# Group norm of a state-space scan: four squared tiles added on GpSimd before TensorE's row sum

## The chip, the cores and the metric

The kernel runs on one core of a Trainium2 chip. The metric is the device time of one execution in microseconds (us). The engines carry the names of the profile: PE is TensorE (matmuls, with weight loads as PEld), DVE is VectorE, ACT is ScalarE, POOL is GpSimd, SP is SyncE. Semaphores are the only thing that orders work on different engines.

## The reference, cut to what matters

The program is two transformer-like blocks on a sequence of 512 tokens of width 1024. The change sits in the second block, in the two-way state-space scan and the gated norm that follows it:

```python
v = (y * jax.nn.silu(z)).astype(jnp.float32).reshape(bsz, s, SSD_GROUPS, d // SSD_GROUPS)
v = v * lax.rsqrt(jnp.mean(v * v, axis=-1, keepdims=True) + EPS)
return (v.reshape(bsz, s, d) * g.astype(jnp.float32)).astype(y.dtype)
```

Here `y` is the scan's output (2048 channels), `SSD_GROUPS` is 4, and so each mean is over the 512 channels of one group. In the kernel channels lie on partitions and tokens along the free axis: a group is four tiles of 128 channels x 512 tokens, and the mean over channels is a sum over four tiles and over the 128 partitions of each.

## The kernel before

All matrix products go through one stream of weight units (128 x 1024). Each unit is split into a high and a low part, by ACT (`split_hi`, L342) and by DVE (`split_lo`, L348), and PE multiplies them in 48 matmuls of 256 columns (`product_tile`, L376).

The scan (`ssd_pe`, `ssd_act`, `ssd_dve`, `ssd_rows_dma`) makes 16 steps, f = 4 g + j, four groups g of four steps j, written out by hand on every engine. In a step PE computes the tiles x and z of step f (96 matmuls of L376), at j = 0 the four matmuls of `c_times_b` (L2376), at j = 1 of groups 1 to 3 `square_sum(g - 1)` (L2364), then `heads(f - 1)` (L2353, L2356), and transposes (L2391). `heads` multiplies with decay matrices in four chunks c, and waits for each.

The decay matrices of a step are made thus: POOL starts eight row copies from DRAM (L2315, four chunks, two heads each), DVE caps them (`cap`, L2492, one instruction per chunk), ACT takes exponentials (L2468, four activations per chunk), and DVE multiplies with a table (`times_cb`, L2498, two instructions per chunk). DVE also does the convolution (L2199), the output `v` (`out`, L2505 and L2508) and the group norm's scaling (L2514). Its order in step f is: convolution, `times_cb(f-1, 3)`, `cap(f, 0)`, `cap(f, 1)`, `split_lo`, `times_cb(f, 0)`, `out(f-1)`, `times_cb(f, 1)`, `cap(f, 2)`, `cap(f, 3)`, `split_lo`, at j = 2 the scaling, `times_cb(f, 2)`. ACT's `exponentials(f, 2)` wait for `cap(f, 2)`.

POOL's order in step f is: the copies of chunks 0 and 1, those of chunks 2 and 3 (each waits for PE to be done with the buffer, L2356), then for f = 1 to 12 the square of tile f - 1 (L2318, which waits for `v` from L2508), then for f = 8 to 15 the low part of the normed tile f - 8 (L2323). The squares of the last group are made on ACT (L2407).

`square_sum(g)` multiplies each squared tile with a matrix of ones and accumulates in one PSUM bank; ACT takes the inverse root there (L2411, L2413).

Of the kernel before, what the change touches and what calls it, by code (L numbers as in the profile page):

```python
# [20 lines left out]
ALU = mybir.AluOpType  # L21
# [176 lines left out]
def build(nc, dram, out):  # L198
    ctx = ExitStack()
    with ctx:  # L200
# [4 lines left out]
        def place(name, first, n, dtype):  # L205
            return first, n, nc.alloc_sbuf_tensor_at(name, [P, n, S], dtype, offset=base + first * S * 4)
        A = Slots(place("big", BIG, RES - BIG, F32), place("res_tmp", RES, N_SLOTS - RES, F32))
# [10 lines left out]
        ps = ctx.enter_context(nc.psum_tensor("ps", [P, 6, S], F32))  # L218
        ident = const[:, CONST["ident"]:CONST["ident"] + P]
        ones = const[:, CONST["ones"]:CONST["ones"] + P]  # L220
# [10 lines left out]
        def sem(name):  # L231
            return ctx.enter_context(nc.semaphore(name))
# [69 lines left out]
        def ev(name):  # L302
            name = SHARED.get(name, (name, 0))[0]
            if name not in s:
                s[name] = sem(name)
            return s[name]

        def nth(name, n):

            return n + SHARED[name][1]  # L310
# [47 lines left out]
        def product_tile(pe, u, t, hi, lo, blocks=(8,), n=S, ready=None, spare=None):  # L358


            pe.wait_ge(acc_free[t.bank], t.in_bank + 1)
            a, k, total = acc[t.bank], 0, sum(blocks)
            parts = [slice(at, at + HALF) for at in range(0, n, HALF)]
            for m in blocks:
                pe.wait_ge(lo_done, u.count + 1)
                for b in range(m):
                    if ready is not None:
                        pe.wait_ge(ev(ready[0]), ready[1] + k + 1)
                    wh = w_hi[:, u.slot, b * P:(b + 1) * P]
                    wl = w_lo[:, u.slot, b * P:(b + 1) * P]  # L370
                    for term, (w, x) in enumerate(((wh, hi), (wh, lo), (wl, hi))):
                        if spare is not None and (k, term) in SETTLE:
                            settle(pe, spare)
                        for h in parts:

                            mm = pe.matmul(a[:, h], w, AR[:, x + k, h], start=(k == 0 and w is wh and x == hi and h.start == 0),  # L376
                                           stop=(k == total - 1 and w is wl), skip_group_check=True)
                    k += 1
                mm.then_inc(units_used, 1)
                u = u + 1  # L380
# [1755 lines left out]
        XT, XTOK, VH, VL = 56, 58, 16, 32  # L2136
# [13 lines left out]
        def rows_buf(b):  # L2150
            return A[:, ROWS + 5 * b:ROWS + 5 * b + 5].rearrange("p b n -> p (b n)")
# [8 lines left out]
        def part(f, b, c):  # L2160
            rows, at = both(f, c)
            return rows[:, b, at:at + S + P]

        def back(f, b, c):
            return part(f, b, c)[:, 0:LENB[c]]

        def fore(f, b, c):
            return part(f, b, c)[:, LENB[c]:S + P]
# [129 lines left out]
        def ssd_rows_dma(pool):  # L2298
            rows = rows_buf(0)
            pool.wait_ge(ev("s_rows"), 8)  # L2300
            for c in range(CH):
                for r, at, n in ((slice(0, 32), FORE[c], LEN[c]), (slice(32, 64), BACK[c], LENB[c])):
                    pool.dma_start(SCR_ROWS[:, at:at + n], rows[r, at:at + n]).then_inc(ev("s_rows_out"), 16)
            pool.wait_ge(ev("s_rows_out"), 2 * CH * 16)
            pool.wait_ge(ev("s_rdiag"), nth("s_rdiag", 1))

            for f in range(SSD_TILES):
                for c in range(CH):

                    before = f - 1 if c < 2 else f  # L2310
                    for b in range(2):
                        if before >= 0:
                            pool.wait_ge(ev("s_pv"), 8 * before + 2 * c + b + 1)
                        src = SCR_ROWS[2 * f + b:2 * f + b + 1, BACK[c]:BACK[c] + S + P].to_broadcast([P, S + P])
                        pool.dma_start(part(f, b, c), src).then_inc(ev(row_in(f, c)), 16)  # L2315
                if 1 <= f <= POOL_SQ:
                    pool.wait_ge(ev("s_v"), f)
                    pool.tensor_tensor(A[:, VH + f - 1], A[:, VL + f - 1], A[:, VL + f - 1],  # L2318
                                       ALU.mult).then_inc(ev("s_vsq"), 1)
                if 8 <= f < 8 + POOL_LO:  # L2320
                    k = f - 8
                    pool.wait_ge(ev("s_vhi"), k + 1)
                    pool.tensor_tensor(AR[:, VL + k], A[:, VL + k], AR[:, VH + k].bitcast(F32),  # L2323
                                       ALU.subtract).then_inc(ev("s_vlo"), 1)


        POOL_SQ, POOL_LO = 12, 8

        def row_in(f, c):
            return f"s_row_in{f % 2}{c}" if c < 2 else f"s_row_in{c}"  # L2330

        def cb_bank(g, c):

            return (3, 4, 5, 0 if g else 1)[c]
# [3 lines left out]
        def ssd_pe(pe):  # L2338
            def heads(f, j, first=False):

                pe.wait_ge(ev("s_xtok"), f + 1)
                if not first or j >= 2:
                    pe.wait_ge(ev("s_v0"), f - 1)

                def x(b, c):
                    return A[:, XTOK + j % 2, c * P + 64 * b:c * P + 64 * b + 64]

                def o(b, lo, hi):
                    return ps[64 * b:64 * b + 64, j % 2, lo:hi]
                for c in range(CH):  # L2350
                    pe.wait_ge(ev("s_w"), 8 * f + (2 * c + 3))
                    for b in range(2):
                        pe.matmul(o(b, c * P, S), x(b, c), fore(f, b, c), start=(c == 0), stop=False,  # L2353
                                  skip_group_check=True)
                    for b in range(2):
                        pe.matmul(o(b, 0, LENB[c]), x(b, c), back(f, b, c),  # L2356
                                  start=False, stop=(c == 3), skip_group_check=True).then_inc(ev("s_pv"), 1)

            def square_sum(g):
                if g < GROUPS - 1:  # L2360
                    pe.wait_ge(ev("s_cb_rest"), 4 * g + 8)
                for k in range(4):
                    pe.wait_ge(ev("s_vsq"), 4 * g + (k + 1))
                    mm = pe.matmul(ps[:, 5], ones, A.at(VH, 4 * g + k), start=(k == 0), stop=(k == 3))  # L2364
                mm.then_inc(ev("s_vsum"), 1)

            def c_times_b(g, first):

                pe.wait_ge(ev("s_bg"), g + 1)
                if first:  # L2370
                    pe.wait_ge(ev("s_bc"), 2 * CH)
                    pe.wait_ge(ev("s_tab"), nth("s_tab", 2))
                for c in range(CH):
                    if c == 3 and not first:
                        pe.wait_ge(ev("s_v0"), 4 * g - 1)
                    pe.matmul(ps[:, cb_bank(g, c)], A[:, BG, c * P:(c + 1) * P], A.at(CT, g), start=True,  # L2376
                              stop=True).then_inc(ev("s_cbt"), 1)

            def group(g, first=False):
                for j in range(4):  # L2380
                    for m in range(2):
                        product_tile(pe, Units(UB["ssd"] + 2 * j + m, g, 8), Tiles(TB["ssd"] + 2 * j + m, g, 8), XH, XL)
                    if j == 0:
                        c_times_b(g, first)
                    if j == 1 and not first:
                        square_sum(g + (-1))
                    if j or not first:
                        heads(4 * g + (j - 1), (j - 1) % 4, first)
                    pe.wait_ge(ev("s_xt"), 4 * g + j + 1)
                    for c in range(CH):  # L2390
                        mm = pe.transpose(ps[:, 2, c * P:(c + 1) * P], A[:, XT + j % 2, c * P:(c + 1) * P], ident)  # L2391
                    mm.then_inc(ev("s_xtt"), 1)
            for g in range(GROUPS):
                group(g, g == 0)

            product_tile(pe, Units(UB["br_ssd"]), Tiles(TB["br_ssd"]), XH, XL)
            heads(SSD_TILES - 1, 3)
            square_sum(GROUPS - 1)

        def ssd_act(act):  # L2400
# [1070 lines left out]
```

## Time and profile before

| | |
|---|---|
| median of 3 runs | 2652.12 us (2649.25 to 2654.46) |
| profiled execution | 2653.07 us, its span 2650.9 us |
| busy, share of the span | PE 97%, DVE 61%, ACT 49%, POOL 4% |
| granted TensorE clock, mean | 0.989 |
| L2364 (square sum) | 32 matmul records of 592 ns |
| L2318 (squares on POOL) | 12 of 1549 ns |
| L2323 (low parts on POOL) | 8, median 1858 ns |

A matmul of 512 columns in this kernel's float32 leaves two records, so L2364's 32 records are 16 matmuls. Records overlap, as matmuls are pipelined: the time of a matmul is read from the start of one to the start of the next. The same holds for DVE, where an instruction starts a little before the one before it has ended. The scan lies between about 1440 and 1751 us of the span.

### The profile page before, as it was taken

What the parts mean: (1) busy time and instruction counts of PE and PEld (TensorE: products, weight loads), DVE (VectorE), ACT (ScalarE), POOL (GpSimd) and SP (SyncE); (2) the same over time, 40 slices, a digit from 0 to 9 for tenths busy, and PEclk for the clock granted to TensorE, in tenths of its full rate; (3) what the DMA queues carried; (4) which work ended last, traced back from release to release, by engine and by line L of the source; (5) the groups of instructions that cost most, each with busy time, mean ns of one, the idle gap of its engine ahead of it and who ended that gap; (6) DMA issues with size and microseconds to landing.
All of it is one profiled execution on the core that took longest, in us unless ns stands there. A gap on an engine that the chain in (4) does not pass through costs nothing.

```text
span 2650.9 us, 51120 instructions
## 1 busy us (share of the span) xinstructions
PE 2566.6 (97%) x20718; PEld 2368.5 (89%) x20718; DVE 1611.5 (61%) x2730; ACT 1295.4 (49%) x2175; POOL 115.2 (4%) x178
## 2 busy tenths in 40 slices
PE   8999999999998999999999998989999999999998
PEld 7976999999995799999989777779966998999998
DVE  6864666643688676664467998952475444544433
ACT  4556344432457554442365888742475333444422
POOL 0000000000000000000001333300000000000000
PEclk9999999999999999999999999999999999999999
DMA  4341233233231123333354666633211331333232
GB/s 166 109 105 19 64 106 102 96 104 104 96 112 49 33 82 101 98 96 120 98 197 136 203 195 193 196 97 100 91 48 62 99 119 54 94 100 95 95 104 72
DMA packets 76187, 279.04 MB, mean 105 GB/s; under 512 B 9802, under 2 KB 12010, under 8 KB 75488
## 3 DMA queue, kind: packets, MB, share of 16 engines
q1 hardware_dynamic: 62112, 217.42, 25.1%
q0 software_dynamic: 13888, 58.88, 7.7%
q8 instruction: 146, 2.39, 0.4%
q14 instruction: 41, 0.34, 0.0%
HBM read 267.03 MB, written 9.24 MB: 104 GB/s over the span
## 4 chain that ended last, share of the span: by engine, by line
PE 80%; DVE 12%; ACT 4%; issue 3%; DMA 1%; POOL 0%; DVEq 0%; SPq 0%; ACTq 0%
PE acc L376 59%; PE acc L565 4%; PE acc L407 3%; PE ps L565 3%; DVE big L2199 2%; DVE res_tmp L2498 1%; PE ps L407 1%; PE acc L2047 1%; DVE big L2829 1%; DVE w_lo L348 1%; DVE big L1851 1%; PE acc L1699 1%; PE ps L753 1%; DMA res_tmp<-scratch_rows 1%; PE ps L1080 1%
## 5 line engine op out<-in xcount | busy, mean ns | idle before, releaser
L376 PE MATMUL acc<-x_split,w_hi 128*128 128x256 f32 x6784 | 1054.6, 278 | 5.4 <-DVE big L2199 3.3
L376 PEld LDWEIGHTS acc<-x_split,w_hi 128*128 128x128 f32 x6784 | 900.8, 189 | 8.0 <-issue 7.4
L342 ACT ACTIVATE w_hi<-w_raw 128x1024 fp32r<-128x1024 f32 x369 | 389.1, 1056 | 562.0 <-PE acc L376 518.9
L376 PE MATMUL acc<-x_split,w_lo 128*128 128x256 f32 x3392 | 662.2, 277 | 0.0
L348 DVE TENSOR_TENSOR w_lo<-w_raw,w_hi 128x1024 fp32r<-128x1024 f32 x369 | 449.9, 1221 | 300.2 <-ACT w_hi L342 300.1
L376 PE MATMUL acc<-big_r,w_hi 128*128 128x256 f32 x3376 | 522.3, 277 | 0.8 <-DVE big_r L2882 0.8
L376 PEld LDWEIGHTS acc<-x_split,w_lo 128*128 128x128 f32 x3392 | 512.4, 188 | 0.0
L376 PEld LDWEIGHTS acc<-big_r,w_hi 128*128 128x128 f32 x3376 | 446.8, 188 | 1.7 <-DVE big_r L2882 0.9
L376 PE MATMUL acc<-big_r,w_lo 128*128 128x256 f32 x1688 | 329.2, 276 | 0.0
L376 PEld LDWEIGHTS acc<-big_r,w_lo 128*128 128x128 f32 x1688 | 254.4, 188 | 0.0
L1378 ACT ACTIVATE res_tmp<-acc,par 128x512 f32<-128x512 f32 x84 | 65.1, 774 | 135.1 <-PE acc L376 130.7
L1403 DVE SCALAR_TENSOR_TENSOR res_tmp<-acc,par,res_tmp 128x511 f32<-128x511 f32 x84 | 62.8, 748 | 87.4 <-ACT res_tmp L1378 87.2
L2468 ACT ACTIVATE res_tmp<-res_tmp 128x256 f32<-128x256 f32 (+3 forms) x192 | 91.1, 551 | 36.4 <-DVE res_tmp L2492 36.3
L2498 DVE TENSOR_TENSOR res_tmp<-res_tmp 128x640 f32<-128x640 f32 x96 | 81.7, 888 | 13.8 <-ACT res_tmp L2468 13.5
L565 PE MATMUL acc<-big_r,w_hi 128*128 128x256 f32 x432 | 78.0, 280 | 8.4 <-issue 8.3
L2199 DVE SCALAR_TENSOR_TENSOR big<-acc,par,big 128x510 f32<-128x510 f32 (+1 forms) x96 | 71.8, 748 | 12.8 <-ACT big L2189 10.1
L407 PE MATMUL acc<-big_r,w_hi 128*128 128x256 f32 x432 | 76.2, 281 | 0.7 <-DVE res_tmp L833 0.7
L565 PEld LDWEIGHTS acc<-big_r,w_hi 128*128 128x128 f32 x432 | 66.0, 190 | 9.4 <-issue 9.4
L1383 ACT ACTIVATE res_tmp<-res_tmp 128x512 f32<-128x512 f32 x44 | 27.9, 633 | 89.6 <-DVE small L1411 89.6
L581 ACT ACTIVATE w_hi<-w_sum 128x512 fp32r<-128x512 f32 x72 | 45.6, 633 | 52.2 <-DVE w_sum L602 52.2
L1406 DVE SCALAR_TENSOR_TENSOR res_tmp<-acc,par,res_tmp 128x510 f32<-128x510 f32 x84 | 62.9, 749 | 11.7 <-DVE res_tmp L1403 0.3
L407 PEld LDWEIGHTS acc<-big_r,w_hi 128*128 128x128 f32 x432 | 65.9, 188 | 1.5 <-DVE res_tmp L833 1.1
(403 smaller groups left out, 3558.5 us busy)
## 6 DMA issues: line engine op xcount, KB each, us to landing
w_raw<-in_stream SPq DMA_DIRECT2D x405, 512.0 KB, 3.5
res_tmp<-scratch_rows POOLq DMA_DIRECT2D x96, 320.0 KB, 5.1
big<-scratch_rows POOLq DMA_DIRECT2D x32, 320.0 KB, 5.7
scratch_bias<-res_tmp POOLq DMA_DIRECT2D x1, 2560.0 KB, 54.5
res_tmp<-in_x SPq DMA_DIRECT2D x2, 1024.0 KB, 6.7
res_tmp<-scratch_bias POOLq DMA_DIRECT2D x8, 256.0 KB, 4.1
scratch_x<-res_tmp POOLq DMA_DIRECT2D x1, 2048.0 KB, 8.0
scratch_kv<-big POOLq DMA_DIRECT2D x1, 2048.0 KB, 7.9
```

The source lines that it names most:

```text
L342: act.activation(w_hi[:, u.slot], w_raw[:, u.slot], ACT.Copy).then_inc(hi_done, 1)
L348: dve.tensor_tensor(w_lo[:, u.slot], w_raw[:, u.slot], w_hi[:, u.slot].bitcast(F32), ALU.subtract).then_inc(lo_done, 1)
L376: mm = pe.matmul(a[:, h], w, AR[:, x + k, h], start=(k == 0 and w is wh and x == hi and h.start == 0), stop=(k == total - 1 and w is wl), ...
L407: mm = pe.matmul(a[:, cols], w, AR[:, x + k, cols], start=(start and k == 0 and w is wh and x == hi), stop=(k == total - 1 and w is wl), s ...
L565: mm = pe.matmul(to, w[:, cols], st_x(stage, f, lo, k), start=(f in (0, 1, 5) and k == n == 0), stop=(k == 3 and n == 2 and f in (3, 5, 6) ...
L581: ins = act.activation(st_form(w_hi, n), x, ACT.Copy)
L1378: act.activation(x, acc[t.bank][:], ACT.Identity, bias=col(f"cb{f}", tile), scale=col(f"cw{f}", tile + 88)).then_inc(ev("conv_now"), 1)
L1403: dve.scalar_tensor_tensor(x[:, 1:S], a[:, 0:S - 1], col(f"cw{f}", tile + 44), x[:, 1:S], ALU.mult, ALU.add).then_inc(ev("conv_tap1"), 1)
L1406: dve.scalar_tensor_tensor(x[:, 2:S], a[:, 0:S - 2], col(f"cw{f}", tile), x[:, 2:S], ALU.mult, ALU.add).then_inc(acc_free[t.bank], 1)
L2199: ins = dve.scalar_tensor_tensor(o, i, col("cw2", m + 24 * j), o, ALU.mult, ALU.add)
L2468: ins = act.activation(w, w, ACT.Exp, bias=tab[:, 0, c, head:head + 1])
L2498: dve.tensor_tensor(w, w, cb, ALU.mult).then_inc(ev("s_w"), 1)
```

## The change

For groups 0 to 2, POOL, after it has squared tile f - 1, adds it to the group's first squared tile (in place), once for the second, third and fourth tile of each group. That is nine more instructions on POOL, each with a wait for POOL's own square. PE's `square_sum` of these groups then is one matmul where it was four. The semaphore `s_vsq` now counts seven steps for such a group (four squares, three sums), and the waits' values follow. The last group stays as it was.

```diff
                 if 1 <= f <= POOL_SQ:
                     pool.wait_ge(ev("s_v"), f)
+                    g, k = divmod(f - 1, 4)
                     pool.tensor_tensor(A[:, VH + f - 1], A[:, VL + f - 1], A[:, VL + f - 1],
                                        ALU.mult).then_inc(ev("s_vsq"), 1)
+                    if k:
+                        pool.wait_ge(ev("s_vsq"), 7 * g + 2 * k)
+                        pool.tensor_tensor(A[:, VH + 4 * g], A[:, VH + 4 * g], A[:, VH + f - 1],
+                                           ALU.add).then_inc(ev("s_vsq"), 1)
...
             def square_sum(g):
                 if g < GROUPS - 1:
                     pe.wait_ge(ev("s_cb_rest"), 4 * g + 8)
+                if g < POOL_SQ // 4:
+                    pe.wait_ge(ev("s_vsq"), 7 * g + 7)
+                    pe.matmul(ps[:, 5], ones, A.at(VH, 4 * g), start=True, stop=True).then_inc(ev("s_vsum"), 1)
+                    return
                 for k in range(4):
-                    pe.wait_ge(ev("s_vsq"), 4 * g + (k + 1))
+                    pe.wait_ge(ev("s_vsq"), 7 * g + (k + 1))
                     mm = pe.matmul(ps[:, 5], ones, A.at(VH, 4 * g + k), start=(k == 0), stop=(k == 3))
                 mm.then_inc(ev("s_vsum"), 1)
```

`POOL_SQ` is 12 and `POOL_LO` is 8. The steps f with an added sum are 2, 3, 4, 6, 7, 8, 10, 11 and 12.

## Rows read from the trace of the kernel before

**Rows 1.** Busy time of each engine (with instruction counts) over the scan.

```profile
1440.00:1751.00 311.00, 290.38 (x2153) 227.06 (x2152) 276.90 (x372) 248.28 (x435) 97.54 (x144) 0.97 0.59 186
```

**Rows 2.** Chain that ended last, within the scan: start us, us, what.

```profile
1529.32 3.43 PE ps L2364 x8
...
1652.69 12.09 PE acc L376 x96
...
1673.26 10.89 PE acc L376 x96
1684.15 3.43 PE ps L2364 x8
...
1693.08 7.10 DMA res_tmp<-scratch_rows
```

**Rows 3.** Waits in the scan: who waited for whom, us in total, times, longest.

```profile
PE ps L2353 <- DVE res_tmp L2498: 20.6, 11, 4.6
...
ACT res_tmp L2468 <- DVE res_tmp L2492: 36.3, 15, 3.0
```

**Rows 4.** Timeline of PE at square_sum(0): start, us, engine line op, form, count.

```profile
1529.16 3.59 PE L2364 MATMUL ps<-big,const 128*128 128x512 f32 x8
```

**Rows 5.** Timeline of PE at chunk 3 of heads(4), heads(8) and heads(12).

```profile
1535.96 0.39 PE L2353 MATMUL ps<-res_tmp,big 128*64 128x128 f32 x4
...
1610.32 0.44 PE L2353 MATMUL ps<-res_tmp,big 128*64 128x128 f32 x4 [0.61 <-DVE res_tmp L2498]
...
1690.80 0.39 PE L2353 MATMUL ps<-res_tmp,big 128*64 128x128 f32 x4
```

**Rows 6.** Timeline of DVE: pairs of times_cb and of cap, without and with POOL beside them.

```profile
1532.13 1.55 DVE L2498 TENSOR_TENSOR res_tmp<-res_tmp 128x640 f32<-128x640 f32 x2
...
1577.85 2.40 DVE L2498 TENSOR_TENSOR big<-big,res_tmp 128x640 f32<-128x640 f32 x2
...
1580.17 1.28 DVE L2492 TENSOR_TENSOR res_tmp<-res_tmp 128x512 f32<-128x512 f32 x2
...
1600.81 2.37 DVE L2492 TENSOR_TENSOR res_tmp<-res_tmp 128x512 f32<-128x512 f32 x2
```

**Rows 7.** Timeline of DVE: times_cb of chunk 3 of step 12.

```profile
1688.31 1.55 DVE L2498 TENSOR_TENSOR res_tmp<-res_tmp 128x640 f32<-128x640 f32 x2
```

**Rows 8.** Timeline of DVE: cap of chunks 2 and 3 in steps 2, 5 and 13.

```profile
1487.95 0.69 DVE L2492 TENSOR_TENSOR res_tmp<-res_tmp 128x512 f32<-128x512 f32 x1 [0.21 <-DMA res_tmp<-scratch_rows]
1489.33 0.69 DVE L2492 TENSOR_TENSOR res_tmp<-res_tmp 128x512 f32<-128x512 f32 x1 [0.69 <-DMA res_tmp<-scratch_rows]
...
1542.94 0.69 DVE L2492 TENSOR_TENSOR res_tmp<-res_tmp 128x512 f32<-128x512 f32 x1 [0.17 <-DMA res_tmp<-scratch_rows]
1544.47 0.69 DVE L2492 TENSOR_TENSOR res_tmp<-res_tmp 128x512 f32<-128x512 f32 x1 [0.85 <-DMA res_tmp<-scratch_rows]
...
1699.14 0.69 DVE L2492 TENSOR_TENSOR res_tmp<-res_tmp 128x512 f32<-128x512 f32 x1
1700.20 0.69 DVE L2492 TENSOR_TENSOR res_tmp<-res_tmp 128x512 f32<-128x512 f32 x1 [0.38 <-DMA res_tmp<-scratch_rows]
```

**Rows 9.** Timeline of POOL: a square, a low part behind a square, a low part alone.

```profile
1578.02 1.55 POOL L2318 TENSOR_TENSOR big<-big 128x512 f32<-128x512 f32 x1 [4.61 <-DVE big L2508]
...
1600.17 1.86 POOL L2323 TENSOR_TENSOR big_r<-big,big_r 128x512 fp32r<-128x512 f32 x1
...
1693.63 1.30 POOL L2323 TENSOR_TENSOR big_r<-big,big_r 128x512 fp32r<-128x512 f32 x1
```

**Rows 10.** Timeline of DVE: out(6), out(7), then out(10), out(11), their first instructions.

```profile
1576.46 0.74 DVE L2505 SCALAR_TENSOR_TENSOR big<-big,par,ps 128x512 f32<-128x512 f32 x1
...
1597.10 0.74 DVE L2505 SCALAR_TENSOR_TENSOR big<-big,par,ps 128x512 f32<-128x512 f32 x1
...
1654.95 0.74 DVE L2505 SCALAR_TENSOR_TENSOR big<-big,par,ps 128x512 f32<-128x512 f32 x1
...
1676.69 0.74 DVE L2505 SCALAR_TENSOR_TENSOR big<-big,par,ps 128x512 f32<-128x512 f32 x1
```

## The prediction

> **What bounds the kernel now.** I read the page first: PE is busy for 97% of the span, so taking matmuls away looks like time won. Then I read the scan alone. There PE is busy for 290.38 of 311 us and DVE for 276.90 [rows 1]: two engines close to full, and the question is which of them ends each step. The chain that ended last goes through both. It holds `square_sum(0)` at 1529.32 and `square_sum(2)` at 1684.15, with 3.43 us each, but nothing of `square_sum(1)` [rows 2]. The list of waits says why: PE waits in `heads` for DVE's `times_cb`, 11 times and 20.6 us in total [rows 3]. In a step that ends in such a wait PE's own speed is worth nothing, DVE's is worth all of it. ACT waits 15 times for DVE's `cap` (36.3 us) [rows 3]; so a delay of `cap(f, 2)` goes on to ACT and comes back in the next exponentials.
>
> **What is removed.** `square_sum` takes 3.43 us for four matmuls, less than the 3.59 us of its row, as the last record's end overlaps the next work [rows 2, 4]. One matmul is 3.43 / 4 = 0.86 us, three are 2.57 us, and three groups 7.7 us. That is the most the change can give. What of it reaches the end is read from chunk 3 of `heads` a few us later, in the same step, where PE meets DVE [rows 5]:
> - heads(4): PE comes at 1535.96 and doesn't wait. DVE was done at 1532.13 + 1.55 = 1533.68 [rows 6]. Cover: 2.28 us.
> - heads(8): PE already waits 0.61 us. Gain: none.
> - heads(12): PE comes at 1690.80, DVE was done at 1688.31 + 1.55 = 1689.86 [rows 7]. Cover: 0.94 us.
>
> What follows on the chain is a row copy that PE's progress releases, and DVE's `cap` behind it: in step 5 DVE waits 0.17 + 0.85 us for copies, in step 13 it waits 0.38 us [rows 8]. An earlier PE can't give back more than these two waits, 1.4 us in all, since DVE is next.
>
> **What is added.** Nine sums on POOL, each right behind a square. POOL itself has time: it waited 4.61 us for the tile before one square [rows 9]. The price is paid on DVE, which is seen in two rows. A pair of `times_cb` takes 1.55 us alone and 2.40 us with a square beside it: 0.85 us lost. A pair of `cap` takes 1.28 us alone and 2.37 us with a low part (L2323) beside it, which comes directly behind a square as the sum will: 1.09 us lost [rows 6]. These rows are also in steps that DVE ends, so I can see that the loss stays: from out(6) to out(7) there are 1597.10 - 1576.46 = 20.64 us with one POOL instruction in the step, and from out(10) to out(11), the same place one group later but with two, 1676.69 - 1654.95 = 21.74 us [rows 10]. The difference is 1.10 us.
>
> The sum has two different inputs and one output of 128 x 512, as the low part has, so I take 1.09 us for it. The bounds: 0.85 us from below (the square, which reads one tile), 1.30 us from above (a low part alone on POOL [rows 9], as if DVE stood still for the whole of it). I exclude a gain, since POOL only gets more to do.
>
> The Trainium skill (page "SBUF — State Buffer", section "Who interferes with whom") says that a DVE instruction with two SBUF inputs contends with a GpSimd instruction that reads SBUF, and that the one issued second is blocked until the other is through. The trace agrees in kind; it speaks against this change, which adds only such instructions. In length the rows say 0.85 and 1.09 us beside POOL records of 1.55 and 1.86 us, less than the whole instruction, and the sum above goes by the rows.
>
> **The sum**, D being how late DVE is:
> - Step 2. `cap(2, 2)` to `cap(2, 3)` is 1.38 us now, as it waits for copies [rows 8]; with a sum beside it it becomes 2.37 - 0.68 = 1.69 us. D = 0.3.
> - Step 3: copies again leave it a little short of full, +1.0; step 4, +1.09. D = 2.4. This meets heads(4): DVE is done at 1533.68 + 2.4 = 1536.1, PE, now 2.57 us early, waits for it, and goes on where it went on before. The first group's saving is gone.
> - Step 5: DVE no longer waits for copies. Its first wait is 0.17 us; the second stretch is 1544.47 - 1542.94 = 1.53 us where 0.60 would do, 0.93 us. D = 2.4 - 1.1 = 1.3.
> - Steps 6, 7, 8 and 10: 4 x 1.09 = 4.36. D = 5.6. `square_sum(1)` saves nothing, by heads(8).
> - Steps 11 and 12: 2.18. At heads(12) DVE is 2.18 us later against PE than now, cover was 0.94, so PE waits although it saved 2.57. In step 13 the copy wait goes: 1700.20 - 1699.14 = 1.06 where 0.60 would do, 0.46 us. D = 5.6 + 2.2 - 0.5 = 7.3.
>
> After the scan PE runs from one product to the next, so D stays. Against the profiled execution: 2653.07 + 7.4 = 2660.5 us. That execution lies 0.95 us above the median of the three runs, and for the median I say 2652.12 + 7.4 = 2659.5 us, +0.28%. With 0.85 us for each sum it is nine times 0.24 less, 5.2 us; with 1.30 nine times 0.21 more, 9.3 us: 2657.3 to 2661.4.
>
> **Edits costed at nothing.** The sum of the last tile is ready in time: the square of step 12 waits for out(11), which is through some 1.5 us after 1676.69 [rows 10]; square and sum are 1.55 + 1.86 us, which gives 1681.6, before PE's 1684.15 [rows 2]. The row copies of chunks 0 and 1 of the next step go out behind the sum, up to 1.86 us later, while DVE is 1.09 us later: they lose 0.8 us. What hides that is that DVE comes to them late: its waits for copies are all at chunks 2 and 3 [rows 8]. If this cover is gone in a step, it costs up to 0.8 us there.
>
> **Rivals.**
> 1. *PE is the bound, as the page says.* Then 7.7 us are won and the sums cost nothing: 2644.4. It decides from the point where DVE has more cover at chunk 3 of heads than 2.57 us plus its delay. Rows 5 show 2.28, none, and 0.94. Chance 0.08.
> 2. *The sums hurt DVE where it has time.* DVE stands idle before each `times_cb(f, 0)`, for ACT. If that wait didn't move with `cap(f, 2)`, it would take up most of D. The result lies between a gain of 1.4 and a loss of 5: 2650.7 to 2657. Rows 10 speak against it, the same-sized second instruction did cost 1.10 us. Chance 0.20.
> 3. *The block is longer than the nearest rows say.* If DVE loses a whole POOL record of 1.55 us per sum, 9 x 0.46 = 4.1 us come on top: 2663.7. It may also come from PE: the longer it waits, the slower what follows; 96 matmuls took 12.09 us at 1652.69, behind a long wait, and 10.89 us elsewhere [rows 2]. At heads(12), now with a wait of 3.8 us, 1.2 us more would use up the step-13 cover and come through in part. Chance 0.13, with 2661.4 to 2664.5. (A block for the whole instruction is what the Trainium skill's section named above says, taken literally.)
> 4. *It doesn't do what it says.* If PE's one wait for `s_vsq` ended late, nothing would be saved on PE; but as that saving comes to nothing anyway, the time would be that of the forecast. It has no chance of its own.
>
> **How the numbers follow.** Forecast 0.59 (2657.3 to 2661.4, likeliest 2659.5), absorbed 0.20, longer 0.13, faster 0.08. The range leaves out the faster case and the lower part of the absorbed one: 2653.5 to 2664.0. A measurement of this kernel can tell about 0.2%, 5.3 us, from no change. Slower by more: the forecast but its lowest edge, and the third rival, 0.70. Same: most of the second rival and that edge, 0.22. Faster: 0.08.
>
> **What would show each step.** L2364 with 14 records (three times 2, once 8) instead of 32. Behind each square of steps 2 to 4, 6 to 8, 10 to 12 a second POOL instruction, about 1.9 us, and beside it a `cap` pair of about 2.4 us. PE's wait at chunk 3 of heads(8) at 3 us or more, and a wait at heads(4) and heads(12), where there is none. DVE's waits for row copies in steps 5 and 13 gone. The step from out(6) to out(7) at 21.7 us instead of 20.64. I am wrong if the `cap` pairs stay short (then the sum costs less), or if they are long and the steps aren't (then there was cover that I didn't see).

## The result and the profile after

The kernel became slower: 2664.09 us median against 2653.13 us, five runs of each; the ratio is 1.0037, with a 95% interval of 1.0025 to 1.005 (6.6 to 13.3 us). I had said 2659.5, +7.4 us.

| | before | after |
|---|---|---|
| profiled execution | 2653.07 us | 2661.63 us |
| its span | 2650.9 us | 2659.8 us |
| first `cap` to out(15) | 303.24 us | 312.45 us |
| matmuls of `square_sum`, groups 0 to 2 | 12 | 3 |
| POOL elementwise instructions | 20 | 29 |

The third row is the best measure of the scan itself: from the start of the first `cap` to the start of `out(15)`, 1444.26 to 1747.50 before and 1442.10 to 1754.55 after. What lies around it scatters by itself: in the twelve profiles of this study the first `cap` stands between 1442.1 and 1450.8 us. The scan grew by 9.21 us. The spans differ by 8.9: the scan's 9.2, less 2.2 for an earlier start of the scan, plus 1.9 behind it.

In the new kernel's lines `cap` is L2501, `times_cb` L2507, `out` L2514, `heads` L2358 and L2361, the square L2319, the sum L2323, the low part L2328, the single matmul L2369.

PE did shed its work. The rows of the single matmul (answers to [rows 4]), which now has six records in all (the last group's eight stand on a line of their own):

```profile
L2369 PE MATMUL ps<-big,const x6: 590/590/591, 1527.1 to 1688.8; 128*128 128x512 f32 x6
```

And PE lost it again at once. Chunk 3 of heads(4), heads(8) and heads(12), the same three places as [rows 5]; in brackets the idle time before it and who ended it:

```profile
1534.12 0.44 PE L2358 MATMUL ps<-res_tmp,big 128*64 128x128 f32 x4 [2.66 <-DVE res_tmp L2507]
...
1613.75 0.44 PE L2358 MATMUL ps<-res_tmp,big 128*64 128x128 f32 x4 [3.00 <-DVE res_tmp L2507]
...
1696.94 0.48 PE L2358 MATMUL ps<-res_tmp,big 128*64 128x128 f32 x2 [3.19 <-DVE res_tmp L2507]
```

Before, these waits were none, 0.61 and none. Over the scan (answers to [rows 3], who waited for whom, us in total, times, longest) PE's waits for DVE went from 20.6 to 32.1 us and ACT's from 36.3 to 40.5:

```profile
PE ps L2358 <- DVE res_tmp L2507: 32.1, 15, 4.5
```

What DVE pays is seen beside the sums. The timeline of DVE and POOL, first step 7 (a square and a sum), then step 8 (square, sum, low part), to be read against [rows 6] and [rows 9]:

```profile
1581.38 2.37 DVE L2501 TENSOR_TENSOR res_tmp<-res_tmp 128x512 f32<-128x512 f32 x2
...
1603.12 3.48 DVE L2501 TENSOR_TENSOR res_tmp<-res_tmp 128x512 f32<-128x512 f32 x2
...
1602.60 1.75 POOL L2323 TENSOR_TENSOR big<-big 128x512 f32<-128x512 f32 x1
1604.32 1.74 POOL L2328 TENSOR_TENSOR big_r<-big,big_r 128x512 fp32r<-128x512 f32 x1
```

A `cap` pair is 1.28 us with no sum or low part beside it, 2.37 with one of them (the sum), 3.48 with both: 1.09 and 1.11 us for each. From out(6) to out(7), the step that was 20.64 us [rows 10]:

```profile
1577.68 0.74 DVE L2514 SCALAR_TENSOR_TENSOR big<-big,par,ps 128x512 f32<-128x512 f32 x1
...
1599.42 0.74 DVE L2514 SCALAR_TENSOR_TENSOR big<-big,par,ps 128x512 f32<-128x512 f32 x1
```

It is 21.74 us now, where the forecast had 21.7. And one thing that I had costed at nothing: the row copies go out behind the sums, and DVE now waits for those of chunk 1, in steps 9, 12 and 13, where it did not before:

```profile
1615.09 0.69 DVE L2501 TENSOR_TENSOR big<-big,res_tmp 128x512 f32<-128x512 f32 x1 [0.80 <-DMA big<-scratch_rows]
...
1674.58 0.69 DVE L2501 TENSOR_TENSOR res_tmp<-res_tmp 128x512 f32<-128x512 f32 x1 [0.61 <-DMA res_tmp<-scratch_rows]
```

In step 13 the wait is 0.99 us. There a second one stands, for chunk 3. It was to go by the forecast, and it grew from 0.38 us [rows 8] to 1.26:

```profile
1707.65 0.69 DVE L2501 TENSOR_TENSOR res_tmp<-res_tmp 128x512 f32<-128x512 f32 x1 [1.26 <-DMA res_tmp<-scratch_rows]
```

### The profile page after: what moved, and what is told of

The parts are those of the page before. It is cut to its first block, busy times and chain, and to the rows that moved or that the text cites. A ratio compares the mean times of both kernels' runs of the same rounds, so it can differ in the third digit from the quotient of the medians.

```text
span 2659.8 us, 51093 instructions
## 1 busy us (share of the span) xinstructions
PE 2564.6 (96%) x20700; PEld 2368.1 (89%) x20700; DVE 1620.8 (61%) x2730; ACT 1296.9 (49%) x2175; POOL 130.6 (5%) x187
## 4 chain that ended last, share of the span: by engine, by line
PE 76%; DVE 13%; ACT 6%; issue 3%; DMA 1%; POOL 0%; DVEq 0%; SPq 0%; ACTq 0%
PE acc L376 57%; PE acc L565 4%; PE acc L407 3%; PE ps L565 3%; DVE big L2199 2%; DVE res_tmp L2507 1%; PE ps L407 1%; DVE res_tmp L2501 1%; PE acc L2047 1%; ACT res_tmp L2477 1%; DVE big L2838 1%; DVE big L1851 1%; DVE w_lo L348 1%; PE acc L1699 1%; PE ps L753 1%
## 5 line engine op out<-in xcount | busy, mean ns | idle before, releaser
L2477 ACT ACTIVATE res_tmp<-res_tmp 128x256 f32<-128x256 f32 (+3 forms) x192 | 91.3, 553 | 40.7 <-DVE res_tmp L2501 40.5
L2507 DVE TENSOR_TENSOR res_tmp<-res_tmp 128x640 f32<-128x640 f32 x96 | 81.3, 883 | 14.6 <-ACT res_tmp L2477 14.2
```

The source lines that it names most:

```text
L2477: ins = act.activation(w, w, ACT.Exp, bias=tab[:, 0, c, head:head + 1])
L2507: dve.tensor_tensor(w, w, cb, ALU.mult).then_inc(ev("s_w"), 1)
```

## The experiments

All runs, with the scan measured as above in the profiled execution. "Against before" is the ratio of times with its interval; the kernels of one block shared a chip and their runs of before. The last column is the scan against 303.24 us. Three kernels leave out a part of the norm's sum (`pe_one_no_sums`, `fill_for_sum`, `half_sums`): they are for timing alone.

| run | median us | against before | scan us | scan, difference |
|---|---|---|---|---|
| changed kernel | 2664.09 | 1.0037 (1.0025 to 1.005) | 312.45 | +9.2 |
| `sums_pe_four` | 2661.47 | 1.0038 (1.0024 to 1.0052) | 310.93 | +7.7 |
| `pe_one_no_sums` | 2653.26 | 0.9998 (0.9989 to 1.0008) | 302.37 | -0.9 |
| `fill_for_sum` | 2653.58 | 1.0000 (0.9991 to 1.001) | 301.53 | -1.7 |
| `copies_first` | 2670.19 | 1.0073 (1.005 to 1.0095) | 319.74 | +16.5 |
| `sums_twice` | 2674.89 | 1.0076 (1.0052 to 1.0101) | 323.10 | +19.9 |
| `act_squares` | 2650.26 | 0.9983 (0.9973 to 0.9993) | 303.31 | +0.1 |
| `act_squares_dve_lows` | 2649.25 | 0.9979 (0.9967 to 0.9992) | 300.14 | -3.1 |
| `before_again` | 2650.27, one run | - | 301.45 | -1.8 |
| `sums_group0` | 2655.92 | 1.0011 (1.0002 to 1.0021) | 305.60 | +2.4 |
| `half_sums` | 2659.95 | 1.0025 (1.0016 to 1.0035) | 308.28 | +5.0 |

**How far the scan can be trusted.** The kernel before, profiled once more:

> The kernel before, once more, for its profile: how much the length of the scan (first cap to out(15)) differs between two executions of the same kernel. If the scan is a good measure, 303.2 within 0.5 us, although the whole span differs by more.

It was 301.45 us, 1.8 less, not within 0.5. 0.7 us of that fall in step 2, where the one execution waited for row copies and the other didn't, and another 0.8 between out(11) and out(12). (`pe_one_no_sums`, which is the same up to step 5, waited 1.65 us for copies in step 2.) Differences of the whole scan below 2 us say nothing; the lengths of single instructions and of steps without a copy wait are good to some hundredths.

**Is PE's saving lost?** The theory is that DVE ends the steps; the rival that PE does. First the sums without the saving:

```diff
-                    pe.matmul(ps[:, 5], ones, A.at(VH, 4 * g), start=True, stop=True).then_inc(ev("s_vsum"), 1)
+                    for k in range(4):
+                        mm = pe.matmul(ps[:, 5], ones, A.at(VH, 4 * g), start=True, stop=True)
+                    mm.then_inc(ev("s_vsum"), 1)
```

> The sums stay on POOL, but PE does four matmuls for each of groups 0 to 2 as before (all four of the summed tile, the last one counts). My theory, that PE's saving is lost because PE waits for DVE at heads(4), (8) and (12): the time of the changed kernel within 0.5 us, about 2664, and the scan (first cap to out(15)) at 312.4 us as there. Rival, that PE's matmuls count: 7.7 us more, 2672.

Giving PE its nine matmuls back cost nothing: 2661.47 against 2664.09 us, the scan 1.5 us shorter. I had said within 0.5 us; the difference is within the scatter, and 0.8 us of it arise in step 13, told further down. The rival's 7.7 us more are ruled out. At heads(4) DVE and PE now come together (the timeline of PE; before the change there was no wait either, after it 2.66 us):

```profile
1536.50 0.44 PE L2358 MATMUL ps<-res_tmp,big 128*64 128x128 f32 x4
```

Then the saving without the sums:

```diff
+                if g < POOL_SQ // 4:
+                    pe.wait_ge(ev("s_vsq"), 4 * g + 4)
+                    pe.matmul(ps[:, 5], ones, A.at(VH, 4 * g), start=True, stop=True).then_inc(ev("s_vsum"), 1)
+                    return
                 for k in range(4):
```

> PE's saving alone: no sums on POOL, and PE sums the rows of the first squared tile alone, so the other three of each of groups 0 to 2 are left out of the norm. My theory: the scan 0 to 1.4 us shorter than before (303.2 us), the time 2651.7 to 2653; DVE's waits for row copies in steps 5 and 13 go. Rival, PE is the bound: 7.7 us shorter, 2645.

The ratio is 0.9998, with an interval that ends 0.11% below 1, so a gain of over 3 us is excluded, let alone 7.7. PE's waits for DVE (list of waits) took up 4.5 us of it, 25.1 where they were 20.6:

```profile
PE ps L2353 <- DVE res_tmp L2502: 25.1, 13, 4.3
```

This run also bears on step 5. The copy waits of [rows 8] there, 0.17 and 0.85 us, are gone: the two `cap` follow each other (timeline of DVE).

```profile
1545.52 1.28 DVE L2496 TENSOR_TENSOR res_tmp<-res_tmp 128x512 f32<-128x512 f32 x2
```

Yet of the 1.02 us only 0.28 came through: from out(4) to out(5) there are 17.00 us before and 16.72 here. That is nearer to the first wait than to both.

**What holds DVE?** Reads on POOL, its queue, or any instruction there:

```diff
-                        pool.tensor_tensor(A[:, VH + 4 * g], A[:, VH + 4 * g], A[:, VH + f - 1],
-                                           ALU.add).then_inc(ev("s_vsq"), 1)
+                        pool.memset(A[:, VH + f - 1], 0.0).then_inc(ev("s_vsq"), 1)
```

> Each sum on POOL becomes a fill of the just squared tile with zeros: POOL still has a second instruction there, with its wait, but it reads no memory; the sum of three tiles is left out. If DVE is held by what POOL reads beside it, the cap pairs go back to 1.3 us and the scan to 302 to 303.5 us, the time to 2653. If it is POOL's queue, which sends the next row copies later, the scan stays a few us longer than 303.2, by as much as the fill is long. If any instruction of POOL holds DVE, the scan stays near 312.

The ratio is 1.0000. The fill takes 0.52 us, and the `cap` pair behind it is back at 1.28 us (timeline of POOL, then DVE):

```profile
1528.22 0.52 POOL L2323 MEMSET big<- 128x512 f32 x1
...
1528.76 1.28 DVE L2500 TENSOR_TENSOR res_tmp<-res_tmp 128x512 f32<-128x512 f32 x2
```

So neither the additional instruction nor its wait costs anything here. That reading is what costs isn't shown by this run alone. The fill is also shorter than the sum, and in all nine places it is over 0.02 us before the next DVE instruction starts; a fill as long as a sum was not run. What speaks against "any work on POOL" is in the kernel before: from 1579.52 on POOL issues row copies, 0.54 us each, and the `cap` pair at 1580.17, beside them, takes its 1.28 us [rows 6].

**How long is the hold?** Sums over half the columns:

```diff
-                        pool.tensor_tensor(A[:, VH + 4 * g], A[:, VH + 4 * g], A[:, VH + f - 1],
-                                           ALU.add).then_inc(ev("s_vsq"), 1)
+                        pool.tensor_tensor(A[:, VH + 4 * g, 0:HALF], A[:, VH + 4 * g, 0:HALF],
+                                           A[:, VH + f - 1, 0:HALF], ALU.add).then_inc(ev("s_vsq"), 1)
```

> The nine sums over the first 256 of 512 columns only; the other half of the norm's sum is left out. If DVE is held for as long as POOL reads, the hold is about half of 1.1 us for each, and the scan 307 to 308.5 us; if the hold has a large fixed part for each instruction, it stays above 309.5; the time 2657 to 2660.

```profile
1504.23 1.19 POOL L2323 TENSOR_TENSOR big<-big 128x256 f32<-128x256 f32 x1
...
1504.75 1.22 DVE L2501 TENSOR_TENSOR res_tmp<-res_tmp 128x512 f32<-128x512 f32 x1
```

The `cap` beside a half sum takes 1.22 us instead of 0.68: 0.54 us lost, against 1.10 (1.78 - 0.68) with a whole sum. It is 0.54 or 0.55 us in all nine places. The hold goes with the columns, and these two sizes show no fixed part in it, although POOL's own record has one (1.19 us for half the columns, 1.75 for all). The Trainium skill (page "GPSIMD Engine Reference", section "3.1 Elementwise — side-by-side cycle accounting") gives 2.6 cycles of a 1.2 GHz clock for each element of a two-input instruction, set by its read port; an estimate from it is 1.11 us for 512 columns and 0.55 for 256. The rows agree in size, 1.10 and 0.54; that DVE is held for just the time in which POOL reads is inferred from this. The square, which has one tile as both its inputs, holds DVE for 0.85 us with the same 512 columns, so the columns alone don't set the hold.

**The dose.** A second sum behind each, into a tile that nobody reads:

```diff
+                        pool.wait_ge(ev("s_vsq"), 10 * g + 3 * k)
+                        pool.tensor_tensor(A[:, VH + f - 1], A[:, VH + 4 * g], A[:, VH + f - 1],
+                                           ALU.add).then_inc(ev("s_vsq"), 1)
```

> Behind each of the nine sums POOL makes a second one into a tile that nobody reads, with its own wait. If each such instruction holds DVE for 1.1 us, the scan is 9 to 11 us longer than the changed kernel's 312.4: 321.5 to 323.5, and the time about 2673. If POOL had cover and the first nine sums only used it up in part, more than that; if DVE's loss came from something once per step (the wait, the order of copies), the scan stays near 312.4.

The scan is 10.65 us longer than the changed kernel's, 2674.89 us in all: 1.18 us for each sum, where the hold is 1.10. Copies may be the rest: DVE's waits for them in the scan are 7.2 us in nine places, where the changed kernel has 3.7 in four.

**The late copies, and a miss.** If the sums delay copies, send these first (the sum goes out of its place behind the square):

```diff
                         pool.dma_start(part(f, b, c), src).then_inc(ev(row_in(f, c)), 16)
+                    g, k = divmod(f - 2, 4)
+                    if c == 1 and 2 <= f <= POOL_SQ + 1 and k:
+                        pool.wait_ge(ev("s_vsq"), 7 * g + 2 * k)
+                        pool.tensor_tensor(A[:, VH + 4 * g], A[:, VH + 4 * g], A[:, VH + f - 2],
+                                           ALU.add).then_inc(ev("s_vsq"), 1)
```

> The same sums, but POOL first sends the row copies of chunks 0 and 1 of the next step and then adds. The changed kernel shows DVE waiting for copies of chunk 1 in steps 9, 12 and 13, which I had costed at nothing; in step 12 it looks as if 0.7 us of it reach the end. If so, these waits go and the scan is 0.7 to 1.5 us shorter than 312.4. If all of the loss is the hold on DVE, the scan stays at 312.4, as the sum then holds split_lo or times_cb in place of cap.

Both expectations missed. The waits for chunk 1 did go (others, at chunks 2 and 3 of steps 6, 13 and 14, came to 3.6 us), but the scan became 7.3 us longer than the changed kernel's. Steps 3, 6, 7, 10 and 11 are 2.1 to 2.2 us longer than before the change, not 1.1; the other steps with a sum 1.1 to 1.7. The timeline (DVE, then POOL) of such a step:

```profile
1505.09 3.48 DVE L2501 TENSOR_TENSOR res_tmp<-res_tmp 128x512 f32<-128x512 f32 x2
...
1502.93 1.55 POOL L2323 TENSOR_TENSOR big<-big 128x512 f32<-128x512 f32 x1 [2.58 <-DVE big L2517]
1504.43 2.16 POOL L2315 DMA_DIRECT2D res_tmp<-scratch_rows  x4
1506.61 1.40 POOL L2319 TENSOR_TENSOR big<-big 128x512 f32<-128x512 f32 x1
```

(L2323 is the square here and L2319 the sum.) Two `cap` are held for 1.1 us each, although there is one sum, and the first of them ends at about 1506.9, with little but the copies' issue beside it: the sum starts at 1506.61. Why a sum that stands behind queued copies holds DVE twice stays open; no run here takes it apart. It does show that here the order on POOL matters, by 7 us.

**The term of step 5.** The sums for group 0 alone:

```diff
-                    if k:
+                    if k and g == 0:
...
-                if g < POOL_SQ // 4:
+                if g == 0:
```

(The waits' values of groups 1 to 3 follow.)

> The sums, and the single matmul, for group 0 alone (steps 2, 3 and 4); groups 1 and 2 as before. The prediction had DVE 1.3 us late once the copy waits of step 5 are used up, since both waits (1.1 us) would cover it. What the changed kernel shows is 2.3 us, since ACT goes on from cap(5, 2) and only that one's wait of 0.17 us covers anything. By the first, the scan is 303.24 + 1.3 - 0.5 = 304.0 us; by the second 303.24 + 2.3 = 305.5 us, less up to 0.5 us at step 13. The time 2655 to 2656.

The scan is 305.60 us. Counted from the first `cap`, `out(5)` is 2.19 us later than before, and it is 2.36 us at `out(15)`. The prediction's value for this point was 1.3 us. The scatter of 1.8 us over a scan would not separate the two, and 0.7 of it falls in step 2. The stretch that the term is about does: from out(4) to out(5) there are 17.00 us in the kernel before, 16.88 in its second profile, 16.72 here and 16.74 in the changed kernel. Step 5 gives back 0.1 to 0.3 us, not 1.1.

**A kernel a little faster than both.** If reads on POOL hold DVE, the squares themselves cost, too, in the kernel before. ACT waits 1.8 to 3.0 us for `cap(f, 2)` in each step from the second on and can make them there:

```diff
-                if 1 <= f <= POOL_SQ:
-                    pool.wait_ge(ev("s_v"), f)
-                    pool.tensor_tensor(A[:, VH + f - 1], A[:, VL + f - 1], A[:, VL + f - 1],
-                                       ALU.mult).then_inc(ev("s_vsq"), 1)
...
                     split_hi(act, ux + 1 + RING)
+                    if 1 <= f <= POOL_SQ:
+                        act.wait_ge(ev("s_v"), f)
+                        act.activation(A[:, VH + f - 1], A[:, VL + f - 1], ACT.Square).then_inc(ev("s_vsq"), 1)
                     exponentials(f, 2)
```

> The kernel before, but ACT makes the twelve squares, just ahead of exponentials(f, 2), where it waits 2 to 3 us for DVE; POOL makes none, and no sums. If reads of POOL beside DVE's two-input instructions are what costs, DVE gets back up to 12 x 0.85 us: the scan 294 to 299 us against 303.2, the time about 2646. If the squares were hidden on POOL, the scan stays at 303 or grows by ACT's 12 x 0.6 us.

The ratio is 0.9983 (0.9973 to 0.9993): faster, but by 0.17%, not by the 10 us that the holds add up to, and the scan of the profiled execution is no shorter at all (at 2658.70 us it was the slowest of the ten; their median is 2650.26). The kernel before had 2655.07 us beside it and 2653.12 and 2652.86 in the other two blocks, and against those two the gain is 0.1%. The list of waits says where the rest went. DVE now waits for row copies, 16.2 us, where it waited 2.3:

```profile
DVE res_tmp L2491 <- DMA res_tmp<-scratch_rows: 16.2, 12, 2.6
```

Then the low parts of groups 0 and 1 to DVE as well, so that POOL only sends copies in the scan:

```diff
-        POOL_SQ, POOL_LO = 12, 8
+        POOL_SQ, POOL_LO = 12, 0
...
-                    if f == POOL_LO:
-                        dve.wait_ge(ev("s_vlo"), POOL_LO)
...
-                    if j == 3 and g > 2:
+                    if j == 3 and not first:
```

> As the one with the squares on ACT, and the eight low parts of POOL are made on DVE too, where one takes 0.6 us of DVE's own time against 1.1 us that one on POOL takes from it: POOL makes no elementwise work in the scan. If so, the scan is 2 to 4 us shorter again. If POOL's low parts were cheaper than DVE's own, it is up to 4.8 us longer.

0.9979 (0.9967 to 0.9992), the scan 300.14 us, 3.2 less than with the squares alone moved; the two times, 2649.25 and 2650.26 us, are not told apart. DVE still waits 15.3 us for copies, in ten places. Their issue waits for PE to be done with a buffer (24 times, 218.6 us), and from there one takes 6.0 us in the middle to land. So it looks as if the copies now end these steps; no run made them faster.

## Why the prediction was right, and where it was off

Direction, cause and bound were right. The time is at the upper edge of the range: 2664.09 us where the range ends at 2664.0. It also lies above the forecast's own 2657.3 to 2661.4, in the band that I had given to the third rival (2661.4 to 2664.5, chance 0.13). The five runs of before lie 1 us above the three that I had (2653.13 against 2652.12); the ratio applied to the latter gives 2661.9. The loss is 11.0 us by the medians, 9.8 by the ratio, 9.2 by the scan, where I had said 7.4. That the last one is so near is luck in part: the profile that I worked from had copy waits in step 2, which a sum could use up. The second profile of the same kernel has none there, and against that one (301.45 us) the scan is 11.0 us longer. A copy wait that differs from one execution to the next is no safe credit.

How late DVE is, step by step, counted from the first `cap` at the start of `out`:

| up to step | predicted | measured | in the step |
|---|---|---|---|
| 2 | 0.3 | 0.47 (1.15 against the second profile) | sum, copy wait taken up |
| 3 | 1.3 | 1.45 | sum |
| 4 | 2.4 | 2.55 | sum |
| 5 | 1.3 | 2.29 | copy waits |
| 6 | 2.4 | 3.38 | sum |
| 7 | 3.5 | 4.48 | sum |
| 8 | 4.6 | 5.15 | sum |
| 10 | 5.6 | 6.29 | sum |
| 11 | 6.7 | 8.10 | sum |
| 12 | 7.8 | 8.73 | sum |
| 15 | 7.3 | 9.21 | copy wait of step 13, grown |

- *What is removed is worth nothing.* Right. At heads(4), (8) and (12) PE waits 2.66, 3.00 and 3.19 us; I had said a wait, 3 or more, and 3.8. `pe_one_no_sums` and `sums_pe_four` show it from both sides.
- *1.09 us for each sum.* Right: 1.10, and steps 3, 4, 6, 7 and 10 grew by 0.98, 1.10, 1.09, 1.10 and 1.12 us. It came from the low part, the only instruction of the trace before with two different inputs that stood behind another on POOL. That I took the nearest row and not the square's 0.85 was worth 2 us of the 9.
- *"DVE no longer waits for copies"* (step 5, a credit of 1.1 us). This step failed, by 0.8 us: 0.26 us came off. The waits did go, but the wait before `cap(5, 3)` covers next to nothing. ACT starts on `cap(5, 2)`, whose own wait is 0.17 us, and it is ACT's exponentials of the next step that DVE waits for in front of `times_cb(6, 0)`. DVE may be done with `cap(5, 3)` 0.85 us sooner and still wait the longer there. The timeline of DVE at `times_cb(6, 0)` has this wait, first in the kernel before, then after:

```profile
1554.51 1.56 DVE L2498 TENSOR_TENSOR res_tmp<-res_tmp 128x640 f32<-128x640 f32 x2
...
1554.46 1.73 DVE L2507 TENSOR_TENSOR res_tmp<-res_tmp 128x640 f32<-128x640 f32 x2 [0.61 <-ACT res_tmp L2477]
```

The time that DVE no longer waits for copies it mostly waits for ACT. `pe_one_no_sums` (0.28 of 1.02 us) and `sums_group0` (0.28) show the size; no run cut the path through ACT. I had written myself that ACT waits for `cap`, and then gave credit for the wrong one.
- *"In step 13 the copy wait goes"* (a credit of 0.46 us). This step failed too, in another way: the wait grew from 0.38 to 1.26 us, and from out(12) to out(15) DVE lost 0.48 us more. The third rival had named the cause. PE had waited 3.19 us at heads(12), and behind it the granted clock was at its lower level of 1.2 GHz (0.51 from 1696.9 to 1700.0); in `sums_pe_four`, where PE waited 2.17 us, it stayed at 2.4 GHz (1.00). The matmuls behind chunk 3, in the changed kernel and then in that run:

```profile
1697.42 1.92 PE L2361 MATMUL ps<-res_tmp,big 128*64 128x512 f32 x4
...
1699.51 1.03 PE L2361 MATMUL ps<-res_tmp,big 128*64 128x512 f32 x4
```

They release the buffer of chunk 3. Counted from the first `cap`, POOL issued that chunk's first copy at 257.55 us, against 256.30 in `sums_pe_four`, which has no wait for it. The clock is not all of it: the chunk's second copy also took 7.25 us from issue to landing, against 5.30. From out(12) to out(13) the one takes 17.42 us and the other 16.60, 0.8 of the 1.5 us by which the two scans differ. (The 12.09 us that the rival went by are of the same kind: PE had waited 3.18 us, and the granted clock was 0.50 from 1648.3 to 1655.1.) It is one execution of each, and their times overlap (2661.63 to 2665.40 and 2661.17 to 2665.11 us), so how often it happens is open.
- *Steps 11 and 12, 2.18 us.* They grew by 1.81 and 0.63. The additional 0.7 of step 11, counted at `out(11)`, which runs in step 12, matches the new wait of 0.61 us for the copy of chunk 1 there. This is the edit that I costed at nothing, with a price of up to 0.8 us "if this cover is gone". I looked at the waits that there were, not at how close the copies of chunk 1 were to becoming one. Steps 11 and 12 together came to 2.44 us for 2.18. That it was this copy is not proved: `copies_first` removed the wait, but brought a larger loss along.
- *Step 8* cost 0.67 and not 1.09. There the sum stands beside `cap(8, 2)`, where the low part stood, and the low part moves to `cap(8, 3)`: for ACT's `exponentials(8, 2)` nothing is later. DVE's wait for ACT before `times_cb(9, 0)`, 1.32 us before, is gone, with the hold of 1.10 us at `cap(8, 3)` and the new copy wait of 0.80 us in its place; which of the two is worth the 0.67 us no run tells. In step 10, with the same three instructions and no copy wait, it was the full 1.12, so the reading is open.
- *The sum is ready in time.* Right, PE never waited for `s_vsq`.
- *The sums hurt DVE where it has time* (second rival). Not seen in step 7, which grew by the full 1.10 us: DVE's wait for ACT before `times_cb(8, 0)` moved with `cap`, 3.08 us before and 3.09 after. It does not stand before each `times_cb(f, 0)`, as the prediction says; steps 3, 6 and 14 of the kernel before have none.
- *The whole-instruction rule* (third rival, 1.55 us each). The hold is 1.10 us beside a record of 1.75, and 0.54 beside one of 1.19. The rule's kind holds, its length doesn't. That the time came out in this rival's band is the work of the credits and the copies above, not of a longer hold.

## What to carry to other kernels

A busy share of 97% doesn't make an engine the bound: go to the place where the engines meet, and read how long the one waits there for the other; that, and not the work removed, is what a saving can bring. An elementwise instruction on POOL that reads tiles in SBUF was paid for by DVE, each time at a `tensor_tensor` with both inputs in SBUF: here 1.10 us for a sum, where an instruction of the same shape on DVE itself takes 0.6 (L2523 of the kernel before, four in 2.49 us), so by these two numbers the work put on POOL "since it is idle" cost DVE more than doing it would have; no run put the sums on DVE. And when a delay is to be covered by a wait, check that the wait is on the path that goes on: of the two waits in a row here, only the one before the instruction that ACT needed counted.

## What the runs showed of the hardware

- DVE's hold beside a two-input instruction of POOL goes with the columns: 0.54 us for 256, 1.10 us for 512. Beside a square of 512 columns it is 0.85 us. A fill on POOL (0.52 us) cost nothing where it stood, and the issue of row copies (0.54 us each) lengthened no `cap` beside it (1.28 us the pair).
- In the steps with a square, DVE finishes the instruction that it is in, and the next one is held: the `times_cb` that starts 0.17 us before the square takes its 0.82 us, the one behind it 1.66.
- A sum that stands behind four row copies on POOL's queue went with two held DVE instructions, 1.1 us each, instead of one. It is unexplained.
- Two executions of the same kernel differ by 1.8 us within a stretch of 303 us, 0.7 of it at waits for row copies.
- Behind a wait of 3.19 us TensorE's granted clock was 0.51 for the next 3.1 us, and four matmul records took 1.92 us; behind one of 2.17 us it was 1.00, and they took 1.03.
